# A decoder block on one core: the four stationary operand tiles stored interleaved

## The reference, cut to what matters

```python
xn = rmsnorm(h, norm_w[l], NORM_EPS)
proj = xn @ w_in[l]                                   # 2048 -> 18432
(rq, rk, rv, rz, dq, dk, dv, dz, g_ret, g_diff) = jnp.split(proj, SPLIT_POINTS, axis=-1)
...                                                   # rotary, retention, differential attention per head
mixed = (jax.nn.sigmoid(g_ret) * (o_ret @ w_ret_up[l])
         + jax.nn.sigmoid(g_diff) * (o_diff @ w_diff_up[l]))
h = h + mixed @ w_out[l]
return rmsnorm(h, final_norm_w, NORM_EPS)
```

## Time and profile before

| | |
|---|---|
| median of 2 runs | 1134.23 us (1133.94 to 1134.52) |
| the profiled execution | 1133.74 us |
| its span, first to last instruction | 1131.8 us |
| TensorE, matmuls | 1111.7 us busy, 98% |
| TensorE, weight loads | 919.7 us busy, 81% |
| VectorE | 612.9 us busy, 54% |
| ScalarE | 519.8 us busy, 46% |
| the 16 DMA engines | 61.6% for the loads and stores of the kernel |
| mean granted TensorE clock | 0.998 |

### The profile page before, as it was taken

One profiled execution on the slowest core, in us unless ns is written; L12 is line 12 of the kernel. 1 busy time (PEld: TensorE's weight loads), 2 busy tenths in 40 slices (PEclk: granted clock), 3 DMA queues, 4 the chain that ended last, 5 costly groups with the idle time before them and its releaser, 6 DMA issues.

```text
span 1131.8 us, 14293 instructions
## 1 busy us (share of the span) xinstructions
PE 1111.7 (98%) x5018; PEld 919.7 (81%) x5018; DVE 612.9 (54%) x729; ACT 519.8 (46%) x673; POOL 47.6 (4%) x62
## 2 busy tenths in 40 slices
PE   6999999999999999999999999999999999999997
PEld 5788888788888888888888888888888888888885
DVE  5655455465544445555645555465556565566544
ACT  5544444444445443344544454445554454444443
POOL 0200000000000000000100001000100010000111
PEclk9999999999999999999999999999999999999999
DMA  9766656666665566666566656665656655565863
GB/s 345 252 186 180 199 155 183 187 183 175 183 182 169 184 192 197 190 187 186 167 176 182 186 164 181 184 187 167 179 168 191 181 176 167 191 187 184 288 205 111
DMA packets 108594, 213.27 MB, mean 188 GB/s; under 512 B 6660, under 2 KB 7688, under 8 KB 107784
## 3 DMA queue, kind: packets, MB, share of 16 engines
q1 hardware_dynamic: 107704, 209.02, 61.6%
q10 hardware_dynamic: 848, 3.68, 0.9%
HBM read 210.58 MB, written 2.10 MB: 188 GB/s over the span
## 4 chain that ended last, share of the span: by engine, by line
PE 96%; DMA 2%; issue 1%; ACT 1%; DVE 0%; ACTq 0%; POOLq 0%; POOL 0%; DVEq 0%
PE bank L879 30%; PE bank L881 30%; PE bank L880 30%; DMA raw<-w_in_dram 2%; PE bank L889 1%; PE bank L899 1%; PE bank L906 1%; PE bank L908 1%; PE bank L986 1%; PE bank L907 1%; DMA mixed<-x_t_dram 0%; PE bank L990 0%; PE bank L1039 0%; PE bank L931 0%; ACT gate L461 0%
## 5 line engine op out<-in xcount | busy, mean ns | idle before, releaser
L590 DVE TENSOR_TENSOR w_lo<-raw,w_hi 128x1024 fp32r<-128x1024 f32 x383 | 474.4, 1240 | 484.1 <-ACT w_hi L392 482.7
L392 ACT ACTIVATE w_hi<-raw 128x1024 fp32r<-128x1024 f32 x383 | 405.8, 1060 | 571.7 <-PE bank L881 556.2
L879 PE MATMUL bank<-w_hi,xt_hi 128*128 128x512 f32 x1280 | 509.1, 398 | 12.5 <-DVE w_lo L656 7.9
L881 PE MATMUL bank<-w_hi,xt_lo 128*128 128x512 f32 x1280 | 499.7, 390 | 0.0
L880 PE MATMUL bank<-w_lo,xt_hi 128*128 128x512 f32 x1280 | 498.9, 390 | 0.0
L879 PEld LDWEIGHTS bank<-w_hi,xt_hi 128*128 128x128 f32 x1280 | 240.9, 188 | 62.2 <-DVE w_lo L656 7.9
L881 PEld LDWEIGHTS bank<-w_hi,xt_lo 128*128 128x128 f32 x1280 | 240.6, 188 | 51.5
L880 PEld LDWEIGHTS bank<-w_lo,xt_hi 128*128 128x128 f32 x1280 | 241.0, 188 | 48.2
L879 PE MATMUL bank<-w_hi,ot_hi 128*128 128x512 f32 x256 | 100.0, 390 | 0.0
L881 PE MATMUL bank<-w_hi,ot_lo 128*128 128x512 f32 x256 | 99.6, 389 | 0.0
L880 PE MATMUL bank<-w_lo,ot_hi 128*128 128x512 f32 x256 | 99.6, 389 | 0.0
(11 more groups left out here) (102 smaller groups left out, 385.1 us busy)
## 6 DMA issues: line engine op xcount, KB each, us to landing
raw<-w_in_dram SPq DMA_DIRECT2D x287, 512.0 KB, 3.7
raw<-w_ret_up_dram SPq DMA_DIRECT2D x32, 512.0 KB, 4.0
raw<-w_diff_up_dram SPq DMA_DIRECT2D x32, 512.0 KB, 4.5
raw<-w_out_dram SPq DMA_DIRECT2D x32, 512.0 KB, 4.5
gate<-x_dram SPq DMA_DIRECT2D x2, 1024.0 KB, 10.6
gate<-x_dram ACTq DMA_DIRECT2D x1, 2048.0 KB, 9.9
out_dram<-mixed SPq DMA_DIRECT2D x8, 256.0 KB, 2.5
mixed<-x_t_dram SPq DMA_DIRECT2D x2, 512.0 KB, 10.4
```

The source lines that it names most:

```text
L392: act.activation(w_hi[:, s, :, :], raw[:, s, :, :], ACT.Copy).then_inc(hi_ready, 1)
L590: dve.tensor_tensor(w_lo[:, s, :, :], raw[:, s, :, :], w_hi[:, s, :, :].bitcast(F32), ALU.subtract) \
L879: pe.matmul(bank[bk][:, :], hi, w_hi[:, s, kk, :], start=k == 0, stop=False)
L881: return pe.matmul(bank[bk][:, :], lo, w_hi[:, s, kk, :], start=False, stop=k == KT - 1)
```

## The change

In each of the four tiles the tokens of several column blocks are interleaved, so that the 128 columns of one stationary operand no longer lie side by side. The step from one column to the next is 4 words (16 bytes) in `xt_hi`, 8 words in `xt_lo`, 32 words in `ot_hi` and 2 words in `ot_lo`. The size of the tiles, the order of the instructions and their number on every engine stay as they are; the writers of the tiles write with the same step, and VectorE reads `xt_hi` and `ot_hi` back with it.

```diff
+        def interleaved(xt, tiles):
+            return xt[:, :, :].rearrange("p k n -> p (k n)") \
+                .rearrange("p (g t k b) -> p g k b t", t=P, k=tiles, b=BLOCKS)
+
+        xt_hi_v, xt_lo_v = interleaved(xt_hi, 2), interleaved(xt_lo, 4)
+        ot_hi_v, ot_lo_v = interleaved(ot_hi, KT), interleaved(ot_lo, 1)
+
+        def stationary(v, k, b):
+            tiles = v.shape[2]
+            return v[:, k // tiles, k % tiles, b, :]
...
-                act.activation(ot_hi[:, bass.ds(head * 2, 2), :],
-                               bank[4 + m % 2][:, :].rearrange("p (k t) -> p k t", k=2), ACT.Copy) \
+                act.activation(ot_hi_v[:, 0, bass.ds(head * 2, 2), :, :],
+                               bank[4 + m % 2][:, :].rearrange("p (k b t) -> p k b t", k=2, b=BLOCKS), ACT.Copy) \
...
-                    last = act.activation(xt_hi[:, k, :], xt_raw[:, k, :], ACT.Copy, scale=norm_col[:, k:k + 1])
+                    last = act.activation(xt_hi_v[:, k // 2, k % 2, :, :],
+                                          xt_raw[:, k, :].rearrange("p (b t) -> p b t", b=BLOCKS),
+                                          ACT.Copy, scale=norm_col[:, k:k + 1])
...
-                        out=xt_lo[:, k, :], in0=xt_raw[:, k, :], scalar=norm_col[:, k:k + 1],
-                        in1=xt_hi[:, k, :].bitcast(F32), op0=ALU.mult, op1=ALU.subtract)
+                        out=xt_lo_v[:, k // 4, k % 4, :, :],
+                        in0=xt_raw[:, k, :].rearrange("p (b t) -> p b t", b=BLOCKS), scalar=norm_col[:, k:k + 1],
+                        in1=xt_hi_v[:, k // 2, k % 2, :, :].bitcast(F32), op0=ALU.mult, op1=ALU.subtract)
...
-                hi, lo = left_hi[:, k, b * P:(b + 1) * P], left_lo[:, k, b * P:(b + 1) * P]
+                hi, lo = stationary(left_hi, k, b), stationary(left_lo, k, b)
                 pe.matmul(bank[bk][:, :], hi, w_hi[:, s, kk, :], start=k == 0, stop=False)
                 pe.matmul(bank[bk][:, :], hi, w_lo[:, s, kk, :], start=False, stop=False)
                 return pe.matmul(bank[bk][:, :], lo, w_hi[:, s, kk, :], start=False, stop=k == KT - 1)
```

More of the change, by code:

```diff
@@ L543, in read_mt_hi @@
                 k = 4 * j + 2 * half
-                act.activation(xt_hi[:, k:k + 2, :], bank[4 + half][:, :].rearrange("p (k t) -> p k t", k=2),
-                               ACT.Copy).then_inc(mt_hi_ready, 1)
+                act.activation(xt_hi_v[:, k // 2, :, :, :],
+                               bank[4 + half][:, :].rearrange("p (k b t) -> p k b t", k=2, b=BLOCKS), ACT.Copy).then_inc(mt_hi_ready, 1)
             def square_h(j, b):
@@ L636, in read_ot_lo @@
                 dve.wait_ge(ot_hi_ready, count + 1)
-                dve.tensor_tensor(ot_lo[:, bass.ds(head * 2, 2), :],
-                                  bank[4 + m % 2][:, :].rearrange("p (k t) -> p k t", k=2),
-                                  ot_hi[:, bass.ds(head * 2, 2), :].bitcast(F32), ALU.subtract) \
+                dve.tensor_tensor(ot_lo_v[:, bass.ds(head * 2, 2), 0, :, :],
+                                  bank[4 + m % 2][:, :].rearrange("p (k b t) -> p k b t", k=2, b=BLOCKS),
+                                  ot_hi_v[:, 0, bass.ds(head * 2, 2), :, :].bitcast(F32), ALU.subtract) \
                    .then_inc(drained[4 + m % 2], 1)
@@ L804, in read_mt_lo @@
                 k = 4 * j + 2 * half
-                dve.tensor_tensor(xt_lo[:, k:k + 2, :], bank[4 + half][:, :].rearrange("p (k t) -> p k t", k=2),
-                                  xt_hi[:, k:k + 2, :].bitcast(F32), ALU.subtract).then_inc(drained[4 + half], 1)
+                dve.tensor_tensor(xt_lo_v[:, k // 4, k % 4:k % 4 + 2, :, :],
+                                  bank[4 + half][:, :].rearrange("p (k b t) -> p k b t", k=2, b=BLOCKS),
+                                  xt_hi_v[:, k // 2, :, :, :].bitcast(F32), ALU.subtract).then_inc(drained[4 + half], 1)
             def add_residual(j, b):
@@ L918, in _ @@
                         pe.wait_ge(xt_lo_ready, u + 1)
-                    unit(n0 + s, u, 2 * (g % 2), xt_hi, xt_lo)
+                    unit(n0 + s, u, 2 * (g % 2), xt_hi_v, xt_lo_v)
                     if s in (10, 12):
@@ L955, in _ @@
                         start_group(2 * g, up_uses(it, 0))
-                    unit(n0 + s, u, 2 * g, ot_hi, ot_lo)
+                    unit(n0 + s, u, 2 * g, ot_hi_v, ot_lo_v)
             pe.wait_ge(lam_sign_step, 2)
@@ L971, in _ @@
                         start_group(banks, diff_uses_high(it, 0) if g == 0 else diff_uses_low(it, (g - 1) // 2))
-                    unit(n0 + s, u, banks, xt_hi, xt_lo)
+                    unit(n0 + s, u, banks, xt_hi_v, xt_lo_v)
                     if s == 12:
@@ L1026, in _ @@
                 if g < GROUPS_D:
-                    unit(U_TAIL + s, u, banks, ot_hi, ot_lo)
+                    unit(U_TAIL + s, u, banks, ot_hi_v, ot_lo_v)
                 else:
-                    unit(U_TAIL + s, u, banks, xt_hi, xt_lo)
+                    unit(U_TAIL + s, u, banks, xt_hi_v, xt_lo_v)
                 if 1 <= g <= GROUPS_D and u == 1:
@@ L1047, in _ @@
                     for kk in range(KU):
-                        mm = three_passes(u, kk, tail_banks(GROUPS_D - 1) + b, b, xt_hi, xt_lo)
+                        mm = three_passes(u, kk, tail_banks(GROUPS_D - 1) + b, b, xt_hi_v, xt_lo_v)
                 mm.then_inc(filled[tail_banks(GROUPS_D - 1) + b], 1)
```

## The result

The changed kernel takes **1190.8 us** (median of 2 runs, 1190.7 to 1190.9) against 1134.23: a ratio of 1.0508 with an interval of 1.049 to 1.0525, slower by 56.6 us. The profiled execution took 1190.7 us, its span is 1188.7, the granted clock 0.999. The forecast of 1327 was far too high; the direction and the place were right.

A forecast was written before the change was run, and what follows sets the result against it. TensorE's matmuls were taken to bound the kernel. Added to 1133.7 us: + 188.4 for loads outlasting matmuls, + 8.0 and 0.2 behind short matmuls, - 3.5 at the start, sum + 193.1; forecast 1327 us, range 1132 to 1355.

The forecast's parts named there:

- The bound and the place: TensorE's matmuls, busy 98% of the span, bound the kernel; only the distance between the 4608 big matmuls can move time much.
- The price of a stepped load: Steps 4, 8, 32: time from one load's start to the next's, behind idle, becomes 0.055 latency + 0.213 reading = 0.27 us.
- rival A: Stepped weight loads stay hidden inside the 0.2267 us between matmuls; 1134 us, at most 1136; chance 0.33.
- The reason for taking the upper end: Moving stream needs 0.2267 us, not 0.2133, for 512 neighbouring words, so is near its read limit; stepped loads have little spare.
- The cover of 0.2267: Loads hide beside a matmul for 0.2267 us; each of 4352 stepped loads exceeds it by 0.0433 us, + 188.4 us.
- Rival B: Hidden loads disturb the moving stream, 0.004 to 0.009 us on 4352 matmuls; 1151 to 1173 us, about 1160; chance 0.10.
- The loads of `ot_lo` stay hidden: The 256 loads with step 2 need 0.16 us, fit in 0.2267, and leave the distance ending at their matmul at 0.227.
- Steps of 8 and 32 cost what 4 costs: Weight loads of `xt_lo` and `ot_hi` are no dearer than step 4, since each word is already read alone.
- Rival C: Steps 8 and 32 dearer still: load takes 0.48 us, 1792 loads add 0.21 us each; 1703 us; chance 0.06.
- Behind short matmuls: Less time to hide loads behind transposes and short matmuls: 68 x 0.117 = + 8.0 us, and 16 places + 0.2.
- The start: Before 36 us TensorE waits for its weights anyway, so its 80-odd lengthened matmuls there cost nothing: - 3.5 us.
- The writers: ScalarE's and VectorE's stepped writes taken at 0 us, at most 2 before the first matmul; step on one side only.

## Why the prediction was wrong

**The bound and the place: right.** 42.5 + 6.5 of the 57 us are in the distance from one of the 4608 matmuls to the next, and the kernel with interleaved tiles and plain loads loses nothing. But the reason that was forecast, a hold longer than the cover, is not there: none behind a wait or a short matmul is longer than 0.216 in the changed kernel.

**The price of a stepped load, 0.055 + 0.213 = 0.27 us: this is the step that failed.** It was built from two parts, and the first was not there. The 0.055 was read as a latency from how the plain hold grows at the lower clock; the whole hold with step 4 is 0.212, at both levels of the clock. That this is the 0.213 of the second part, 128 columns cost what 512 neighbouring words cost, is luck: 512 cycles would be 0.427 at the lower clock, where it holds 0.212 too. With 0.212 the same accounting gives: each load hidden in the 0.2267, 85 places behind short matmuls dearer by 0.10, some 1142 us. That is close to rival A and 49 us too low. So the mis-sized term alone does not explain the result.

The reason for taking the upper end failed as well. It read the 0.0133 us that a matmul takes over its 512 cycles as a stream close to what its reads can deliver. Such an excess would shrink with the words. It is 13.4 ns at 512 columns, 16.6 at 480 (216.6 - 200.0) and 16.1 at 448 (202.8 - 186.7). And the 388 against 389 ns that were to clear the loads are durations whose end is modelled.

**The cover of 0.2267 as something that is either enough or not: the second fault.** Two things are missing in it. Loads that follow one another beside a stream of 320 columns need longer than one behind a wait: 0.2333 against 0.212 with step 4, 0.2415 against 0.216 with step 8, 0.2265 against 0.201 with step 32. Behind four transposes, with hardly a stream beside it, the first load of the changed kernel holds 0.213. The timeline of that place, against the earlier trace rows:
```profile
44.76 0.31 PEld L896 LDWEIGHTS bank<-w_hi,xt_hi 128*128 128x128 f32 x1
44.98 0.33 PEld L897 LDWEIGHTS bank<-w_lo,xt_hi 128*128 128x128 f32 x1
...
45.22 0.41 PE L897 MATMUL bank<-w_lo,xt_hi 128*128 128x512 f32 x1
```
This load follows others too, and none of the 85 behind short matmuls in this trace holds more than 0.216. So following another load is not what slows it; that points to the stream. But at 512 columns the loads with step 4 last no longer than behind a wait (309 ns), so what in the stream does it stays open. And loads that are hidden hold up the stream: + 25.5 us for step 2 alone. In the changed kernel a matmul stands 11.9 ns later on `xt` and 8.5 on `ot` (6.7 for step 2 everywhere, 18 for step 8), where I had 43 for 4352 of them. How much of that at steps 4 and 8 is a load that comes late and how much a stream held up is not shown.

**Rival B (0.10) was the nearest**: distances of 0.23 to 0.24, which is what was forecast as its sign. Its size, 4 to 9 ns, was taken from a disturbance that dies away; the real one is 11.9 on `xt` and 8.5 on `ot`, and the time is above the 1151 to 1173 of this rival. It ended at 1160, which is the time of step 2 everywhere, and the changed kernel has wider steps.

**The loads of `ot_lo` stay hidden: right, and it did not help.** The timeline of the first up projection in the changed kernel:
```profile
406.24 0.39 PE L897 MATMUL bank<-w_lo,ot_hi 128*128 128x512 f32 x1
406.24 0.19 PEld L898 LDWEIGHTS bank<-w_hi,ot_lo 128*128 128x128 f32 x1
406.47 0.40 PE L898 MATMUL bank<-w_hi,ot_lo 128*128 128x512 f32 x1
```
The load still takes 0.19 by its duration, yet the distance to L898's matmul, which depends on it, is 233.7 ns on the mean of the 256, not 227. The sign I had written down for "a step of 2 is too wide as well" was all three distances longer, and that is what stands here. The word "too wide" would be wrong: the load is in time.

**Steps of 8 and 32 cost what 4 costs: wrong, both ways.** 8 costs more (244.6 against 235.0), 32 about as much (236.6). Rival C's sign seemed to come for 8, and its mechanism was not there, since 16 and 32 are cheaper again and the hold with 8 is 0.216, not 0.48.

**Behind short matmuls: + 8.0 and 0.2 forecast, + 8.6 measured**, 85 places instead of 84, at 0.10 each instead of 0.117. **The start: - 3.5 forecast**; 2.1 us of waiting fell away, and the later first matmul took 0.8 of them. **The writers: nothing in the total, right**; that a step on one side of them costs nothing was wrong, since their durations are up by half to double; only with step 2 it nearly holds.

**The cited rules against these holds.** The kernels with plain loads and with steps of 2, 3 and 4 show holds of 108, 116, 165 and 212 ns. The Trainium skill, "SBUF — State Buffer", in the note on cachelines, asks for at least two hits on a line of 16 bytes; the step of 2 has them, and its load keeps its pace nearly (116), so the trace agrees as far as the load is meant. It gives no hint of the + 2.3% that the same step costs beside 512 columns. The Trainium skill, "Vector Engine (DVE) Microarchitecture Reference", on the SBUF access granule, wants adjacent pairs; put on a load, step 2 should have been as dear as step 4, and 116 against 212 says no. The Trainium skill, "TensorE: Matmul & The Clock Gate", states under "Step-by-step: what each phase is for" that TensorE has two read ports and that loading the next weights does not take read bandwidth from the running matmul. Whether it is bandwidth that the stream loses no run here shows; but that the load beside it is free does not hold in the trace of step 2 everywhere, where the load is in with 0.11 us to spare by its hold and the matmul is 6.7 ns later.

## What to carry to other kernels

Keep the 128 columns of a stationary float32 operand side by side where the moving operand has 512 columns: every step tried (2, 4, 8, 16 and 32 words, and 3 in the loads alone) costs 2 to 7% of this kernel, which is bound by its matmuls, and a step of 2 does so although its load looks perfectly hidden. Do not argue from "it fits in the cover" alone: read the hold behind an idle stretch, then measure it again in a chain with shorter matmuls, and look at the distance from matmul to matmul, which is where the price shows. A step on the writers' side costs nothing here, as the writers are covered, so if a tile must be interleaved for somebody, let the writer or the other reader have the step and not the weight load.

## What the runs showed of the hardware that I had not expected

- Up to step 4 a stepped load costs by groups of four words touched: 116, 165 and 212 ns for 64, 96 and 128 of them, 1.5 ns each on 20. With step 4 it is 212 at either level of TensorE's clock. The plain load follows the clock, 108 and 165, and at the lower level steps 2 and 3 are near it, 170 and 171.
- Among loads that touch 128 such groups the step matters: 212 (4), 216 (8), 199 (16), 201 (32). In a chain, beside 320 columns: 0.2333, 0.2415 and 0.2265 us for 4, 8 and 32.
- A load well inside its cover delays the running stream, by an amount that depends on the stream's length: 0.7, 1.9 and 6.7 ns for step 2 at 448, 480 and 512 columns. It does not go by the load's length: step 3 costs the same 6.7 at 512. Why is open.
- With steps of 4 words and more ScalarE writes a float32 tile at about 1 ns more for each element of the row, and VectorE, which reads and writes with steps, takes as much more: 494 to 753 and 478 to 746 ns for 256, 579 to 1137 for 512. With step 2 it is 516, 480 and 617.
